# Order of the score products of a pair of heads: four 128-row products first, then the four 64-row rotary ones with the heads in turn

## The reference, cut to what matters

```python
q = concat([q[..., :128], apply_rope(q[..., 128:], cos, sin)])        # 192 wide, per head
k = concat([k_nope, broadcast(apply_rope(k_rope))])                   # 192 wide
for qb in range(2):                                                   # query blocks of 128
    q0, kend = qb * 128, qb * 128 + 128
    s = einsum('bqhd,bkhd->bhqk', q[:, q0:kend], k[:, :kend]) * scale
    p = softmax(where(mask, s, NEG_INF))
    out = einsum('bhqk,bkhd->bqhd', p, v[:, :kend])
```

## Time and profile before

| | |
|---|---|
| median of 3 runs | 1715.92 us |
| span of the profiled execution | 1713.6 us |
| mean granted TensorE clock | 0.998 |
| PE busy | 1694.1 us, 99% of the span |
| PEld busy (overlaps PE) | 1398.8 us |
| DVE busy | 973.7 us |
| ACT busy | 813.4 us |
| POOL busy | 88.1 us |
| HBM traffic | 180 GB/s over the span |
| 128-row score products (L452) | 64 records, 183.3 to 443 us |
| 64-row score products (L453) | 64 records, 183.8 to 444 us |

### The profile page before, as it was taken

The page is one execution under the profiler, slowest core; times in us unless marked ns, Lnnn a source line. Parts: engine busy times, 40 slices in busy tenths (PEclk is TensorE's granted clock), DMA queues, the critical chain, the costliest instruction groups (busy, mean ns, idle before and its releaser), DMA issues.

```text
span 1713.6 us, 23822 instructions
## 1 busy us (share of the span) xinstructions
PE 1694.1 (99%) x7808; PEld 1398.8 (82%) x7808; DVE 973.7 (57%) x1154; ACT 813.4 (47%) x1061; POOL 88.1 (5%) x154
## 2 busy tenths in 40 slices
PE   8999999999999999999999999999999999999997
PEld 6888887888888888887878888888888888888886
DVE  5546776767886557564446554454445545554453
ACT  6555554545545444554445544444444444344343
POOL 4100100001000000000000000000000000000000
PEclk9999999999999999999999999999999999999999
DMA  6865555455566655554435566666666666565563
GB/s 213 271 196 168 164 160 147 142 157 153 166 208 182 194 193 174 185 185 152 141 123 179 188 188 191 181 184 190 196 195 185 189 189 188 198 209 190 177 214 123
DMA packets 161295, 309.64 MB, mean 181 GB/s; under 512 B 10323, under 2 KB 16577, under 8 KB 160992
## 3 DMA queue, kind: packets, MB, share of 16 engines
q1 hardware_dynamic: 159168, 302.55, 57.2%
q0 software_dynamic: 1776, 6.47, 1.0%
q10 hardware_dynamic: 304, 0.01, 0.0%
HBM read 306.89 MB, written 2.10 MB: 180 GB/s over the span
## 4 chain that ended last, share of the span: by engine, by line
PE 98%; ACT 1%; DMA 1%; DVE 0%; issue 0%; ACTq 0%; POOL 0%; SPq 0%; DVEq 0%
PE acc L339 29%; PE acc L341 29%; PE acc L340 29%; PE tp L351 3%; PE sc L453 1%; PE sc L452 1%; PE sc L626 1%; PE acc L525 1%; PE acc L527 1%; PE acc L526 1%; PE ov L645 0%; PE acc L505 0%; PE acc L507 0%; PE acc L506 0%; PE ov L471 0%; PE xt L645 0%
## 5 line engine op out<-in xcount | busy, mean ns | idle before, releaser
L1162 DVE TENSOR_TENSOR w_lo<-raw,w_hi 128x1024 fp32r<-128x1024 f32 (+3 forms) x592 | 710.0, 1205 | 606.8 <-ACT w_hi L718 603.1
L718 ACT ACTIVATE w_hi<-raw 128x1024 fp32r<-128x1024 f32 (+3 forms) x592 | 606.8, 1027 | 802.3 <-PE acc L341 770.2
L339 PE MATMUL acc<-w_hi,crossT 128*128 128x512 f32 x832 | 327.4, 394 | 0.0
L341 PE MATMUL acc<-w_hi,crossT 128*128 128x512 f32 x832 | 324.1, 390 | 0.0
L340 PE MATMUL acc<-w_lo,crossT 128*128 128x512 f32 x832 | 324.0, 389 | 0.0
L339 PE MATMUL acc<-w_hi,mixT 128*128 128x512 f32 x800 | 318.2, 398 | 3.3 <-DVE w_lo L1162 2.5
L341 PE MATMUL acc<-w_hi,mixT 128*128 128x512 f32 x800 | 312.8, 391 | 0.0
L340 PE MATMUL acc<-w_lo,mixT 128*128 128x512 f32 x800 | 312.6, 391 | 0.0
L339 PEld LDWEIGHTS acc<-w_hi,crossT 128*128 128x128 f32 x832 | 156.2, 188 | 32.8 <-issue 0.7
L341 PEld LDWEIGHTS acc<-w_hi,crossT 128*128 128x128 f32 x832 | 156.2, 188 | 32.7
L340 PEld LDWEIGHTS acc<-w_lo,crossT 128*128 128x128 f32 x832 | 156.3, 188 | 32.3 <-issue 0.7
(11 more groups left out here) (224 smaller groups left out, 1258.5 us busy)
## 6 DMA issues: line engine op xcount, KB each, us to landing
raw<-in_w_in_dram SPq DMA_DIRECT2D x104, 512.0 KB, 3.7
raw<-in_w_gate_dram SPq DMA_DIRECT2D x88, 512.0 KB, 4.4
raw<-in_w_up_dram SPq DMA_DIRECT2D x88, 512.0 KB, 3.7
raw<-in_w_down_dram SPq DMA_DIRECT2D x80, 512.0 KB, 4.1
raw<-in_w_kv_mem_dram SPq DMA_DIRECT2D x64, 512.0 KB, 3.8
raw<-in_w_o_dram SPq DMA_DIRECT2D x32, 512.0 KB, 3.7
raw<-in_w_q_mem_dram SPq DMA_DIRECT2D x32, 512.0 KB, 3.7
raw<-in_w_o_mem_dram SPq DMA_DIRECT2D x32, 512.0 KB, 3.7
```

Source lines behind the costliest of these rows:

```text
L339: mm(o, lo, whi, start=first and k == 0, stop=False)
L341: ins = mm(o, hi, whi, start=False, stop=end)
L718: fn(w_hi[:, s, 0:width], raw[:, s, 0:width], ACT.Copy).then_inc(hi_done, 1)
L1162: V.tensor_tensor(w_lo[:, s, 0:width], raw[:, s, 0:width], w_hi[:, s, 0:width].bitcast(F32), ALU.subtract).then_inc(lo_done, 1)
```

## The change

In step t = 2 PE's loop is taken apart. First come the four 128-row products: head 0's two blocks, then head 1's. Then come the four 64-row products: the 128-column block of head 0, that of head 1, then the 256-column block of head 0 and that of head 1. Neighbours in this second run thus lie on different halves of the array's rows and in different PSUM banks. Only the first 128-row product of each bank carries the start flag; the second finds its columns unwritten since that flag, and the 64-row ones add. Each head's last product raises `scores_ready`, so the counts that ACT and DVE wait for are doubled. Products, operands and results are the same in number and size.

```diff
+                    blocks = ((0, P, 0), (P, TOK, P))
                     for h in range(2):
-                        r0 = h * ROPE
-                        for qs, keys, at in ((0, P, 0), (P, TOK, P)):
-                            o = sc[:, h, at:at + keys]
-                            mm(o, qnT[:, h, qs:qs + P], knT[:, h, 0:keys], start=True, stop=False)
-                            ins = mm(o, qrT[r0:r0 + ROPE, qs:qs + P], krT[r0:r0 + ROPE, 0:keys],
-                                     start=False, stop=True)
-                    ins.then_inc(scores_ready, 1)
+                        for qs, keys, at in blocks:
+
+                            mm(sc[:, h, at:at + keys], qnT[:, h, qs:qs + P], knT[:, h, 0:keys],
+                               start=qs == 0, stop=False, skip_group_check=True)
+                    for qs, keys, at in blocks:
+                        for h in range(2):
+                            rows = slice(h * ROPE, (h + 1) * ROPE)
+                            ins = mm(sc[:, h, at:at + keys], qrT[rows, qs:qs + P], krT[rows, 0:keys],
+                                     start=False, stop=True, skip_group_check=True)
+                            if qs == P:
+                                ins.then_inc(scores_ready, 1)
...
-                        act.wait_ge(scores_ready, p)
+                        act.wait_ge(scores_ready, 2 * p)
...
-                    dve.wait_ge(scores_ready, p + 1)
+                    dve.wait_ge(scores_ready, 2 * p + 2)
```

## The result

The changed kernel takes 1700.2 us (median of 4 runs, 1699.72 to 1701.46) against 1715.8 for the kernel before beside it (1715.41 to 1716.06): a ratio of 0.9913, with a 95% interval of 0.9901 to 0.9925, or 15.6 us less. The forecast was 1704.5 in a range of 1701 to 1709, so the direction was right and the gain, 11.4 us, too small. The profiled span went from 1713.6 to 1698.2 us, by 15.4; the clock stayed at 0.998.

What follows compares the result with a forecast made beforehand. PE was taken to bound the kernel. Grouping products by shape (-9.7 us) and overlapping the heads (-1.7), with increments at nothing, summed to -11.4: from the median 1715.92 to 1704.5 us, range 1701 to 1709.

Steps and rivals of the forecast that it cites:

- What bounds the kernel: PE, busy 99% of the span: a microsecond it doesn't spend comes off the end, unless another engine makes it wait.
- Part 1: Score products grouped, 128-row then 64-row: six of eight shape changes go, 0.20 us each, -9.7 us over 8 pairs.
- Part 2: Heads in turn in the 64-row run: some records run beside each other on different rows, taken as -1.7 us.
- rival c: In the 64-row run the two heads lie wholly beside each other, -5.1 us, giving 1701.1 us; chance 0.05.
- Part 3: One more semaphore increment a pair, on head 0's last product: costed at nothing, at most 0.03 us a pair.
- What may take it back: Waits on other engines: nothing lost; DVE's score wait falls from 12.2 to about 2 us, exponentials stay 2.4 us ahead.
- e: The time doesn't come through, as another engine holds PE or the next wait takes it: within 3.4 us; chance 0.05.
- rival f: Slower: PE's clock falls behind the 64-row run, 2.2 us a pair, giving 1722.3 us; chance 0.04.
- Rival d: A change of head in the 64-row run costs part (1708.7 us, chance 0.10) or all (1711.1, 0.05) of a shape change.
- Rival b: No overlap in the 64-row run, changes of head free: 2.97 us a block, 1706.2 us; chance 0.25.

## Why the prediction was wrong

**What bounds the kernel: right.** 1.82 us a pair left PE, 14.5 in all, and 14.8 came off between the first block and the end.

**Part 1, 0.20 us a change and six changes away: right in kind, 0.4 us too large.** Two kernels that differ by two changes give 0.40 (3.02 and 2.62), two more changes give 0.39. With both heads on the same rows only the six changes are gone, and the block went from 4.18 to 3.02: 1.16 us a pair, 9.3 in all, where the sum had 9.7. The difference is a misreading of the earlier trace rows. The start of the next product (203.29) was taken as the end of the twelve records, but that product comes early and takes longer itself; the plain distance of its kind is 0.17, and the one behind it shows the true end:

```profile
203.54 0.33 PE L526 MATMUL acc<-w_lo,cqT 128*128 128x384 f32 x1
203.71 0.34 PE L527 MATMUL acc<-w_hi,cqT 128*128 128x384 f32 x1
```

So twelve records take 203.54 - 202.03 - 0.17 = 1.34 us, 0.111 each and not 0.105. A pair without changes takes 8 x 0.111 + 8 x 0.216 = 2.62, which is what the run with all rows measured, and a change costs (4.18 - 2.62) / 8 = 0.195. The change of bank within the 128-row run cost nothing that can be read, as assumed: 1.31 us from its start to the next group with no change behind it, which is the 4 x 0.111 + 4 x 0.216 of its records.

**Part 2, the heads beside each other: the term that was mis-sized.** It stood at -1.7 us and measured -5.3 (same rows against different rows). The failed step was "if starts keep program order only the second record of one can lie beside the first of the next", and the tighter one, that loads go one at a time. In the changed kernel two loads start within 0.01 us on the two halves, and with head 0's two products ahead in the program head 1's first still started with head 0's first. Each half of the rows works through its own records, 6 units beside 6 for 12, in 0.66 us. The tighter step rested on rows in which all loads were for overlapping rows; they could say nothing on disjoint ones. This was rival c, "heads wholly beside each other", at 1701.1 us with a chance of 0.05; I had held against it that the two records of a product are in order. They are, on each half; that order doesn't bind the other half. The estimate by the Trainium skill ("TensorE: Matmul & The Clock Gate", Part 3) for whole products, -5.1 us, agrees with the 5.3 measured; the other one that the prediction took from it, -3.4, doesn't. The same section's sentence that matmuls start in program order doesn't agree with the run that put head after head: head 1's first record starts 0.01 us after head 0's first, ahead of head 0's other three.

**Part 3, semaphores: right.** Nothing measurable for the second increment. The 26 ns an increment by the Trainium skill ("TensorE: Matmul & The Clock Gate", The cost: per-tile semaphore tail) don't show in PE's block; on DVE, where the prediction looked for them, they can't be read, since DVE comes after the scores.

**What may take it back: right in kind.** DVE became the later one at the scores in pair 1 already, not only in pair 7, as scores came 0.4 us earlier than forecast, so its wait fell to nothing and not to 2 us; the reserve of 2.4 us before the turns held, and no wait took the place of the old one. The mean granted clock stayed at 0.998 and e didn't occur; nor did rival f. The lower clock in it was read off the products' distances at the start (0.43 against 0.23 us); the profile's granted clock doesn't show it there, as it reads 1.00 for 10 to 14 us. Rival d falls, as the order with one change of head (2.37) and those with three (2.36) have the same block. Rival b, no overlap, is what the same rows gave: 3.02 where it had 2.97.

**The range.** Its lower end, 1701, was rival c's time, 1701.1. With 5.3 for 1.7 in the sum the forecast would have been 1700.9, and with 9.3 for 9.7 as well 1701.3. So the measured parts alone would have ended just inside the range. Of the 1.1 us from there to 1700.2, the two spans show 0.6 ahead of the first score block, where nothing was changed, and 0.3 behind it. The part ahead moves by as much and more from run to run (2.2 us over all runs here), and I had left no room for that below the last case. That the result fell below 1701 hangs on this scatter; that Part 2 is three times too small does not. What lies around the span is 1700.04 - 1698.2 = 1.8 us and not 2.3; the forecast doesn't hang on it, as it is the median less the gain.

## What to carry to other kernels

Where products over 128 rows alternate with products over 64, count the changes in the timeline: here each cost 0.20 us in 32-bit code, half of it an array that runs empty, half a load with nothing beside it; gather products by shape until one change in and one out are left. Put independent half-height products on both halves of the rows and near each other in the program: here they cost half. When a bound depends on a rule of order that no row shows, keep the case without the rule at an honest chance, and let the range go past the last case by the scatter of the run.

## What the runs showed of the hardware that I had not expected

- Two 64-row streams on disjoint rows and different banks run at full speed beside each other, weight loads included: 0.66 us for about 1.3.
- A half of the rows can start work that stands later in the program: past the rest of four records on the other half at once (0.01 us later), but with eight records ahead only after 0.77 us, when the other half was at its sixth load.
- A small one: a 64-row product isn't cheaper than a 128-row one by itself. The block took 2.62 us with all its products on all rows, and 3.02 with the 64-row ones on one half; the 0.40 are the two changes. So products made full height, with zeros in the other half, should beat alternation (4.18), though not two halves beside each other (2.36). That kernel was not run: the one measured lets each head add the other's rotary part.
